# First norm: first weights ahead of x's second block, its turns behind the first products, identity turns on TensorE

## The reference

```python
h = _rms(x, attn_norm_g[l])        # y = x * rsqrt(mean(x * x) + EPS) * g
proj = h @ w_in[l]                 # (512 x 2048) @ (2048 x 6144): q | k | v | B | C | xc
q, k, v, cb, cc, cx = jnp.split(proj, splits, axis=-1)
...                                # differential attention, short convolution
x = x + jnp.concatenate([a, c], axis=-1) @ w_out[l]
x = x + _peer(_rms(x, ffn_norm_g[l]), peer_w_q[l], peer_subkeys[l], peer_u[l], peer_v[l])
```

## Time and profile before

| | before |
|---|---|
| median of 3 runs | 2966.29 us |
| the profiled execution | 2965.18 us |
| its span, first to last instruction | 2963.4 us |
| TensorE busy | 2892.9 us, 98% |
| VectorE, GpSimd, ScalarE busy | 80%, 51%, 35% |

### The profile page before, as it was taken

One profiled execution on the slowest core, in us unless ns is written; L12 is line 12 of the kernel. 1 busy time (PEld: TensorE's weight loads), 2 busy tenths in 40 slices (PEclk: granted clock), 3 DMA queues, 4 the chain that ended last, 5 costly groups with the idle time before them and its releaser, 6 DMA issues.

```text
span 2963.4 us, 40377 instructions
## 1 busy us (share of the span) xinstructions
PE 2892.9 (98%) x14993; PEld 2571.4 (87%) x14993; DVE 2356.5 (80%) x3050; ACT 1049.3 (35%) x1373; POOL 1510.2 (51%) x906
## 2 busy tenths in 40 slices
PE   8999999999999999999999999999999999999998
PEld 6888777888889999999999999999997788777777
DVE  6455677755688888988888898899777999998898
ACT  4122343341323333434333343334233333333333
POOL 1000232300016666665665666566867778877852
PEclk9999999999999999999999999999999999999999
DMA  8998777779658998999999899999999999999998
GB/s 297 332 348 278 253 237 252 226 289 332 225 187 305 320 340 302 337 320 330 309 322 337 305 339 316 333 343 356 338 348 395 412 415 410 417 418 419 419 417 357
DMA packets 324223, 980.65 MB, mean 331 GB/s; under 512 B 62756, under 2 KB 179504, under 8 KB 240752
## 3 DMA queue, kind: packets, MB, share of 16 engines
q1 hardware_dynamic: 179488, 508.60, 46.5%
q0 software_dynamic: 107008, 439.75, 41.3%
q10 hardware_dynamic: 37584, 30.43, 3.2%
HBM read 866.33 MB, written 112.33 MB: 330 GB/s over the span
## 4 chain that ended last, share of the span: by engine, by line
PE 66%; DVE 15%; DMA 10%; issue 4%; ACT 3%; POOL 1%; ACTq 0%; DVEq 0%; SPq 0%; POOLq 0%
PE ps L1827 21%; PE ps L1829 20%; PE ps L1828 20%; DMA v_two<-in_peer_v 9%; DVE x_rows L1685 3%; PE ps L2079 3%; DVE u_row L1676 2%; DVE v_lo L1725 2%; ACT v_hi L1196 2%; DVE x_one L1775 1%; DMA v_ring<-in_peer_v,experts 1%; DVE uT_lo L1670 1%; DVE uT_lo L1665 1%; PE ps L1910 1%; PE ps L1926 1%
## 5 line engine op out<-in xcount | busy, mean ns | idle before, releaser
L1827 PE MATMUL ps<-hT_hi,uT_hi 128*128 128x384 f32 x2048 | 699.0, 341 | 10.5 <-DVE uT_lo L1665 8.6
L1829 PE MATMUL ps<-h2T_lo,uT_hi 128*128 128x384 f32 x2048 | 686.1, 335 | 0.0
L1828 PE MATMUL ps<-hT_hi,uT_lo 128*128 128x384 f32 x2048 | 684.9, 334 | 0.0
L831 POOL DMA_INDIRECT gate_grid<-gates,grid_cells x256 | 541.5, 2115 | 107.4 <-issue 78.8
L1827 PE MATMUL ps<-v_hi,a_hi 128*128 128x512 f32 x1024 | 405.7, 396 | 31.5 <-DVE v_lo L1725 30.7
L1828 PE MATMUL ps<-v_hi,a_lo 128*128 128x512 f32 x1024 | 402.5, 393 | 0.0
L1829 PE MATMUL ps<-v_lo,a_hi 128*128 128x512 f32 x1024 | 402.3, 393 | 0.0
L1827 PEld LDWEIGHTS ps<-hT_hi,uT_hi 128*128 128x128 f32 x2048 | 384.7, 188 | 19.4 <-DVE uT_lo L1665 14.6
L1196 ACT ACTIVATE v_hi<-v_two 128x2048 fp32r<-128x2048 f32 x126 | 241.3, 1918 | 448.1 <-PE ps L1829 324.9
L1828 PEld LDWEIGHTS ps<-hT_hi,uT_lo 128*128 128x128 f32 x2048 | 385.0, 188 | 1.9
L1829 PEld LDWEIGHTS ps<-h2T_lo,uT_hi 128*128 128x128 f32 x2048 | 384.3, 188 | 0.0
(11 more groups left out here) (209 smaller groups left out, 4975.9 us busy)
## 6 DMA issues: line engine op xcount, KB each, us to landing
v_two<-in_peer_v SPq DMA_DIRECT2D x63, 2048.0 KB, 11.8
u_tile<-in_peer_u SPq DMA_DIRECT2D x72, 1024.0 KB, 8.0
u_tile<-uT_all SPq DMA_DIRECT2D x56, 1024.0 KB, 6.8
near_rows<-in_peer_u SPq DMA_DIRECT2D x40, 1024.0 KB, 8.3
uT_all<-near_turned SPq DMA_DIRECT2D x100, 256.0 KB, 7.0
w_raw<-in_w_in SPq DMA_DIRECT2D x24, 1024.0 KB, 9.3
wc_raw<-in_w_in SPq DMA_DIRECT2D x48, 512.0 KB, 6.6
far_rows<-in_peer_u SPq DMA_DIRECT2D x16, 1024.0 KB, 9.4
```

Source lines behind the costliest of these rows:

```text
L831: pool.indirect_dma_start(out=gate_grid, out_offset=bass.IndirectOffsetOnAxis(ap=grid_cells[:, d, col:col + 1], axis=0), in_=gates[:, 2 + ...
L1827: mm(out, a_hi, b_hi, start=first, stop=False)
L1828: mm(out, a_lo, b_hi, start=False, stop=False)
L1829: return mm(out, a_hi, b_lo, start=False, stop=last)
```

## The change

SyncE asks for the first weights behind the gains, ahead of x's block 1. ScalarE and VectorE split them before block 0's halves; VectorE first waits until block 0 is turned. Squares, mean and scaling of block 1 come behind. VectorE scales block 3 ahead of the second quarter's split. TensorE turns the identity 36 times, turns block 0, turns the identity 24 times into a part of bank 0, and does the first quarter for block 0; block 1 is turned behind it, with block 2, and block 3 ahead of the second quarter for block 0.

```diff
                 sp.dma_start(x_rows[:, t, :], x_v[t]).then_inc(x_in[t], 16)
                 if t == 0:
                     sp.dma_start(gains[0], attn_norm_g[0:1, :].to_broadcast([P, D])).then_inc(gain_in, 16)
-                elif t == 1:
                     load_quarter(w_in_v, 0, 0, range(4))
@@ ScalarE
             square(0, 0)
+            split_wi(0, 0)
+            high(0, 0)
             square(0, 1)
-            high(0, 0)
-            split_wi(0, 0)
             square(0, 2)
             high(0, 1)
             square(0, 3)
@@ VectorE
             mean(0, 0)
             scale(0, 0)
+            dve.wait_ge(hT_ps, 1)
+            split_wi(0, 0)
+            low(0, 0)
             mean(0, 1)
             scale(0, 1)
-            low(0, 0)
-            split_wi(0, 0)
             mean(0, 2)
             scale(0, 2)
             low(0, 1)
             mean(0, 3)
+            scale(0, 3)
             split_wi(0, 1)
-            scale(0, 3)
             low(0, 2)
             low(0, 3)
@@ TensorE
+            def turn_ident(times):
+
+                for _ in range(times):
+                    turn(ps[:, 0, 0:P], ident[:, :], ident[:, :])
+
             pe.wait_ge(const_step, 8)
+            turn_ident(36)
             turn_rows(0, 0)
-            turn_rows(0, 1)
+            turn_ident(24)
             pe.wait_ge(w_ready, 1)
             pe.wait_ge(hT_ready, 4)
             qkv_quarter(0, 0, 0)
+            turn_rows(0, 1)
             turn_rows(0, 2)
             pe.wait_ge(hT_ready, 8)
             qkv_quarter(0, 0, 1)
+            turn_rows(0, 3)
             pe.wait_ge(w_ready, 2)
             qkv_quarter(0, 1, 0)
-            turn_rows(0, 3)
             qkv_quarter(0, 1, 1)
```

## The result

The changed kernel has a median of 2972.16 us over 20 runs (2968.39 to 2978.97), the kernel before 2965.15 us over 20 runs beside it (2960.91 to 2969.27): 7.0 us more, a ratio of 1.0025 with a 95% interval of 1.0018 to 1.0032. The forecast was 2972.0, 5.7 above the median of 2966.29 known then. The profiled execution of the changed kernel took 2968.39 us, span 2966.6, and is the quickest of its 20, only 3.2 over the profiled one of the kernel before; so a difference of two single profiles says less than the medians, and the start is what they are read for.

The account below looks back on a forecast made before the run. TensorE, busy 98% of the span, was taken to bound the kernel, so the start's loss reaches the end: order 3.7 + clock 2.0 = 5.7 us on the 2966.3 median gives 2972.0, range 2969.0 to 2976.5.

Parts of the forecast that it names:

- weights late or level lost twice: Start: weights at 12.7 add 0.9, first stand's lost clock 1.1, on top of 5.7; 2974.0 us, chance 0.27.
- the chain: Start, step by step across engines: second quarter's products of block 1 start at 39.2, not 35.47; 3.7 us later.
- The cost of the order, 3.7: Start: new lists make TensorE wait, 3.3 us of it ahead of block 3's turns; 3.7 us lost overall.
- The weights' landing, 11.8: Start, SyncE's queue: first weights, asked for ahead of block 1, land at 11.8 us, between 11.3 and 16.5.
- The clock, 2.0: TensorE's stand ahead of block 3's turns loses the upper clock level; 2.0 us, bounded by nothing and 3.4.
- Do turns raise the rate?: Start, TensorE: whether identity turns alone bring the upper clock level; the forecast leaned to yes, block 0 turned by 13.4.
- The rival built on it: Start: turns don't raise TensorE's rate, first products held up; 9.6 us slower, 2975.9 us, chance 0.13.
- The gain of faster products, 2.4: First quarter's 12 products for block 0 run at the upper clock level after identity turns; 2.4 us gained.
- the account of the prediction: TensorE's start: gains 2.8 and 2.4 against 1.8 for later turns and 6.9 of waits; a loss of 3.5 us.
- Carried to the end: From the start to about 797 us: the start's loss passes on at full size, nothing later taking it up.

Follow-up runs that it names:

- a sibling: Changed kernel with block 3's turns moved back behind the second quarter's products of block 0; +5.7 us over the kernel before, ratio 1.0018.
- the changed kernel's second profile: Changed kernel run once more with no further edit, beside the kernel before; 2972.71 us against 2966.12, ratio 1.0022.
- the quickest version: Kernel before with identity turns in TensorE's stands and GpSimd's ten small loads moved behind its four powers; 2963.68 us against 2965.94.

## Why the prediction was right

**The hit is partly luck.** 2972.0 was forecast and 2972.16 measured. But the forecast was a loss of 5.7 on top of 2966.3, the median of three runs; beside the changed kernel the kernel before has 2965.15 over 20 runs, and the loss is 7.0. A base 1.1 too high and a loss 1.3 too small cancel. As a loss, the result lies between the forecast, 5.7, and the case "weights late or level lost twice", 7.7. At the start, which the chain was about, 5.7 is met: 5.25 and 6.2 in two profiles.

**The cost of the order, 3.7:** right in size. With all stands filled the second quarter's products of block 1 start at 39.40, where the chain had 39.2; that is 3.8 by M and 4.5 by the medians. Its steps stood where the chain had them: block 2's turns waited for block 1's lower halves, and TensorE stood 3.44 us ahead of block 3's turns (3.3 predicted). That VectorE's list makes this stand and TensorE's order only places it, is shown by turning block 3 behind: a stand of 2.7 stayed. About 2 us belong to block 3's place in the two lists, the rest to the early weights with block 1's late turns.

**The weights' landing, 11.8:** 0.65 too early; ScalarE takes them up at 12.45 and 12.46 in the two profiles of the changed kernel, at 13.35 in that of a sibling. The first products came at 19.3, not 18.65. The error hardly reaches the end, since another one works against it: VectorE went from the start of the split to block 1's lower halves in 10.75 us (14.51 to 25.26 with all stands filled), where the chain has 11.25 (13.8 to 25.05). Of the 0.65, 0.2 is left at 39.40. That a later landing than this is one of the end at full size was right (loads in the old order: landing 4.3 later, M 4.3 to 5.3 later).

**The clock, 2.0:** the sum is right in size, its terms are not. The forecast let one stand cost the level, the one ahead of block 3, for 2.0, and put the first at nothing (1.1 in the rival case). The first, 3.3 us long since the weights were late, cost the level in both profiles: block 2's turns start at 27.20 and 26.95, at 26.09 with the stands filled, which is 0.9 to 1.1. The one ahead of block 3 cost it in one of the two: from block 3's turns to the second quarter for block 1 are 6.2 us there (35.51 to 41.71) and 4.96 in the other (35.76 to 40.72), so 1.2 and not 2.0. By M the two profiles lose 1.3 and 2.3; filling all stands gives back 2.1 by the medians.

**Do turns raise the rate?** The rows of before only showed that they hold it. Two runs settle it: 36 identity turns in 5.91 us with block 0 turned in 1.97 behind them, and a granted clock of 0.50 that rose to 1.00 behind 16 turns alone, with the loads swapped in the kernel before. Here the Trainium skill (TensorE: Matmul & The Clock Gate, Part 4, PE-mode transpose), which says that full rate doesn't engage for turns, doesn't agree with the measurement, and the measurement decides. The rival built on it fell with it.

**The gain of faster products, 2.4,** was counted right in the account but must not be read as what identity turns are worth: without them the changed kernel is 1.0 slower by the medians, and put into the kernel before they bring 0.7, both within the intervals (1.3 to 2.3 and 0.7 by M). The chain had that in it (block 2's turns wait for VectorE), the account of the prediction hid it in its list of waits.

**Carried to the end:** that the start's loss passes at full size to about 797 us is shown. The first turns of the second norm start at 791.52 before, and in the other profiles their difference is that at M within 0.04 us, but for the changed kernel's second profile (6.46 and 6.15). From there on it blurs. The second norm's turns before, then in the changed kernel:

```profile
795.49 2.36 PE L1821 MATMUL ps<-ident,h_rows 128*128 128x128 f32 x16 [0.31 <-DVE h2T_lo L1266]
...
803.35 2.36 PE L1821 MATMUL ps<-ident,h_rows 128*128 128x128 f32 x16 [0.61 <-DVE h2T_lo L1266]
```

```profile
796.69 3.65 PE L1821 MATMUL ps<-ident,h_rows 128*128 128x128 f32 x32
801.01 2.36 PE L1821 MATMUL ps<-ident,h_rows 128*128 128x128 f32 x16 [0.67 <-DVE h2T_lo L1265]
...
809.62 1.91 PE L1821 MATMUL ps<-ident,h_rows 128*128 128x128 f32 x16
```

The second group of turns comes 4.32 us behind the first and not 3.97, in every version with the changed lists and in none with the old ones; no run shows why. The third comes 12.93 behind and not 11.83: 0.35 are the same, the rest goes with a fall of the clock in between (a granted 0.51 from 806 to 809 us). That fall does not belong to the changed lists. It is there in the kernel before with identity turns (0.57 from 800 to 803 us), and missing in the changed kernel without them, where the third group comes 12.19 behind. Behind 800 us single executions wander by more than the steps in question: at 791 us the changed kernel's first profile is 5.2 late, at the end 3.2; the quickest version's is 1.3 early there and 2.2 late at the end. So the 0.4 and 1.8 us by which the changed kernel's medians exceed the difference at M stay open.

## What to carry to other kernels

Where several engines pass a block on, write down each engine's list with its durations before moving a step: the sum of the engine that feeds the rest (here VectorE) decided, and a step moved ahead on one engine only moved its neighbours' waits. Here a load moved ahead was worth something only to lists that ask for it first, and those lists paid each microsecond of its lateness. Fillers that kept TensorE's rate paid where a stand was followed by products that nobody else held up: 2.1 us in the changed kernel, 0.7 in the kernel before. And compare like with like: the price of an order is read from two versions that both have their stands filled.

## What the hardware showed that I had not expected

A stand does not cost the clock each time: the same program lost the level behind its 3.4 us stand at 32 to 35.5 us in one execution and kept it in the other. 16 turns alone, in 3.65 us behind a stand of 7 us, raised the granted clock from 0.50 to 1.00. And ten transfers of 0.2 to 32 KB, issued by GpSimd, held the large ones down to 51 GB/s in a microsecond in which, with them gone, 430 GB/s passed. With them in place 1 MB of weights landed at 16.5 us, without them at 13.6.
